# Two weights loaded earlier, residual rows in four pieces and reordered last tiles in an output projection

## The reference, cut to what matters

```python
# end of the first block
merged = jnp.einsum('bsnd,nbsd->bsd', gates, proj)      # three gated branches
out = merged @ w_out[l]                                 # 1024x1024 by 1024x1024
x = x + rms_norm(out, post_norm_w[l])                   # norm over the features
# start of the second block
n = rms_norm_2(h, attn_norm_w[l])
proj = n @ w_in[l]                                      # 1024x1024 by 1024x2816
aq, ak, av, rq, rk, rv, rg = jnp.split(proj, split_at, axis=-1)
aq = rope(rms_norm_2(aq.reshape(B, S, ATTN_HEADS, HEAD_DIM), q_norm_w[l]), pos)
ak = rope(rms_norm_2(ak.reshape(B, S, ATTN_KV_HEADS, HEAD_DIM), k_norm_w[l]), pos)
```

## Time and profile before

| | us |
|---|---|
| median of three executions | 2512.16 |
| the profiled execution | 2513.58 |
| its span, first to last instruction | 2511.6 |
| PE busy, share of the span | 2433.8 (97%) |
| ACT, POOL, DVE busy | 775.0, 847.7, 1072.5 |
| output projection, first matmul to the end of `early(0,1)` | about 1184.8 to 1311.9 |

### The profile page before, as it was taken

The page is one execution under the profiler, slowest core; times in us unless marked ns, Lnnn a source line. Parts: engine busy times, 40 slices in busy tenths (PEclk is TensorE's granted clock), DMA queues, the critical chain, the costliest instruction groups (busy, mean ns, idle before and its releaser), DMA issues. The chain is left out here.

```text
span 2511.6 us, 44136 instructions
## 1 busy us (share of the span) xinstructions
PE 2433.8 (97%) x18612; PEld 1936.5 (77%) x18612; DVE 1072.5 (43%) x1320; ACT 775.0 (31%) x1219; POOL 847.7 (34%) x502
## 2 busy tenths in 40 slices
PE   7999999999999999899989999989999999999999
PEld 6777777777778888687768887767768888887887
DVE  5544222222222334543473537653487666660000
ACT  5332222222221111432351115532453333332210
POOL 1233111111111212243453441064355554555621
PEclk9999999999999999999999999999999999999999
DMA  6336333332131121243432330021513222224431
GB/s 203 125 126 190 87 86 87 86 86 78 49 100 44 57 60 44 91 140 105 153 132 68 92 99 26 14 102 60 168 59 99 85 67 86 94 70 158 146 116 67
DMA packets 258456, 238.82 MB, mean 95 GB/s; under 512 B 35888, under 2 KB 218416, under 8 KB 258160
## 3 DMA queue, kind: packets, MB, share of 16 engines
q1 hardware_dynamic: 251856, 224.80, 28.7%
q10 hardware_dynamic: 6432, 11.54, 1.7%
HBM read 166.80 MB, written 61.90 MB: 91 GB/s over the span
## 5 line engine op out<-in xcount | busy, mean ns | idle before, releaser
L177 POOL TENSOR_TENSOR wlo<-wraw,whi 128x1024 fp32r<-128x1024 f32 x89 | 223.8, 2516 | 701.9 <-ACT whi L172 688.4
L3308 PE MATMUL tl_ps_bank<-tl_dn,tl_hid 128*128 128x512 f32 x792 | 194.4, 390 | 0.0
L172 ACT CAST whi<-wraw 128x1024 fp32r<-128x1024 f32 x89 | 93.2, 1048 | 324.6 <-PE ring L199 127.9
L3308 PEld LDWEIGHTS tl_ps_bank<-tl_dn,tl_hid 128*128 128x128 f32 x792 | 149.1, 188 | 31.1
L2837 POOL TENSOR_TENSOR tl_oplo<-tl_raw,tl_ophi 128x512 fp32r<-128x512 f32 x66 | 106.9, 1621 | 134.4 <-ACT tl_ophi L2832 134.4
L2837 POOL TENSOR_TENSOR tl_oplo<-tl_sum,tl_ophi 128x512 fp32r<-128x512 f32 x88 | 119.5, 1369 | 72.0 <-ACT tl_ophi L2832 72.0
L2845 PE MATMUL tl_ps_bank<-hT_lo,tl_ophi 128*128 128x512 f32 x352 | 113.2, 393 | 2.1 <-POOL tl_oplo L2837 2.1
L2845 PE MATMUL tl_ps_bank<-tl_M,tl_ophi 128*128 128x512 f32 x352 | 112.2, 390 | 0.0
L1023 DVE COPY_PREDICATED rs_X<-rs_level,rs_ps_bank 128x512 f32<-128x512 int32 x40 | 29.6, 739 | 191.4 <-PE rs_ps_bank L1054 191.4
L1075 PE MATMUL lead<-hT_hi,whi 128*128 128x512 f32 x230 | 103.1, 448 | 3.4 <-DVE rs_f_out L989 2.2
L3230 DVE TENSOR_TENSOR tl_res<-lead,tl_res 128x512 f32<-128x512 f32 x4 | 2.8, 692 | 231.5 <-PE lead L3308 231.5
(11 more groups left out here) (499 smaller groups left out, 6219.4 us busy)
## 6 DMA issues: line engine op xcount, KB each, us to landing
wraw<-in_w_in SPq DMA_DIRECT2D x79, 512.0 KB, 4.1
scratch_pg<-rs_f_out SPq DMA_DIRECT2D x48, 256.0 KB, 2.4
wraw<-in_w_out SPq DMA_DIRECT2D x24, 512.0 KB, 4.0
tl_raw<-in_w_gate SPq DMA_DIRECT2D x11, 1024.0 KB, 6.9
tl_raw<-in_w_up SPq DMA_DIRECT2D x11, 1024.0 KB
scratch_hid<-tl_H SPq DMA_DIRECT2D x11, 1024.0 KB, 4.9
tl_hidraw<-scratch_hid SPq DMA_DIRECT2D x22, 512.0 KB, 3.3
tl_dnraw<-in_w_down SPq DMA_DIRECT2D x44, 256.0 KB, 2.8
```

The source lines that it names most:

```text
L172: self.nc.scalar.copy(self.hi[s][:, :], self.raw[s][:, :]).then_inc(self.hi_ready, 1)
L177: self.nc.gpsimd.tensor_tensor(self.lo[s][:, :], self.raw[s][:, :], self.hi[s][:, :].bitcast(F32), ALU.subtract).then_inc(self.lo_ready, 1)
L3308: ins = nc.tensor.matmul(bank[b][:, :], hid[k][:, x, c], dn[n % 2][:, v, :], start=k == 0 and j == 0, stop=k == FF - 1 and j == 2)
```

## The change

It has five parts. (a) `phase_merge` ends with SP loading weight tiles 2 and 3 of the output projection, behind its own last transfers and a wait for its last weight split; `phase_out` begins its loads with tile 4. (b) The residual rows come in four DMAs of 1 MB, one behind each of the weight loads 5 to 8, and POOL waits for all four. (c) ACT evicts tiles 14 and 15 ahead of the casts of weights 16 and 17 (before, only 15), and the chain of slices 4 to 7 stands at t = 14 and 15 instead of 13 and 14. (d) On PE `early(0,0)` waits for each slice of its data instead of for all eight; the sums of the second half stand behind its sixth slice instead of the fourth, the transposes `back(2,1)` behind the second slice of `early(1,0)`; in `early(0,1)` the sum of squares stands ahead of the three matmuls of its slice, and `back(3,0)` ahead of the last slice. (e) In `phase_in2` the waits for the tables move from the start to T = 2 on DVE and behind the second split on POOL.

```diff
--- before.py
+++ after.py
@@ -1550,6 +1550,7 @@
     N, SLOTS = 3 * KD, 4
     with ExitStack() as ctx:
         sh = Shared(nc, ctx, "mg")
+        w.phase(sh)
         b_dram = d.w_branch.rearrange("n (k p) c -> n p k c", p=P)
         piece = lambda t, s: t[:, s * HALF:(s + 1) * HALF]
         raw = [piece(w.raw[s // 2], s % 2) for s in range(SLOTS)]
@@ -1589,6 +1590,9 @@
                         weights(t + SLOTS)
                     if t + 2 < N:
                         gate(t + 2)
+                sp.wait_ge(wl, N)
+                for t in (2, 3):
+                    w.load(sp, t, t % 2, columns(d.w_out, t))
 
             @block.gpsimd
             def _(pool):
@@ -1732,6 +1736,7 @@
         back_ps = [sh.ps(f"back{h}", [P, HALF]) for h in range(2)]
         sum1_ps = [sh.ps(f"sum1{h}", [P, HALF]) for h in range(2)]
         stat = [slice(h * NB, (h + 1) * NB) for h in range(2)]
+        chain = lambda t: {11: (0, 1), 12: (2, 3), 14: (4, 5), 15: (6, 7)}.get(t, ())
         copied, squared, added, summed, root, step, scaled, x1_ready, x_in, stored = (
             sh.sem(n) for n in "copied squared added summed root step scaled x1_ready x_in stored".split())
         widened, returned, squared1, added1, summed1, x1_hi, x1_lo, rms_ready, rms_sum = (
@@ -1740,10 +1745,11 @@
 
             @block.sync
             def _(sp):
-                for t in range(2, N + len(following)):
+                for t in range(4, N + len(following)):
                     w.load(sp, t, t % 2, columns(d.w_out, t % KD) if t < N else following[t - N])
-                    if t == 4:
-                        sp.dma_start(x[:, :, :], d.xT.rearrange("k p s -> p k s")).then_inc(x_in, 16)
+                    if 5 <= t < 9:
+                        k = 2 * (t - 5)
+                        sp.dma_start(x[:, k:k + 2, :], d.xT[k:k + 2].rearrange("k p s -> p k s")).then_inc(x_in, 16)
                 for k in range(KD):
                     sp.wait_ge(x1_ready, KD + k + 1)
                     sp.dma_start(d.x1T[k], x1[:, k, :]).then_inc(stored, 16)
@@ -1754,7 +1760,7 @@
                 def residual(h, k):
                     pool.wait_ge(scaled, h * KD + k + 1)
                     if not k:
-                        pool.wait_ge(x_in, 16)
+                        pool.wait_ge(x_in, 64)
                     nc.gpsimd.tensor_tensor(x1[:, k, half[h]], x1[:, k, half[h]], x[:, k, half[h]], ALU.add).then_inc(x1_ready, 1)
 
                 for t in range(N):
@@ -1792,16 +1798,15 @@
                     nc.scalar.activation(sq1[k % 2] if h or k else total1, x1[:, k, half[h]], ACT.Square).then_inc(squared1, 1)
 
                 for t in range(N):
-                    if t == N - 1:
+                    if t >= N - 2:
                         evict(t)
                     w.split_hi(act, t + 2, t % 2, t // 2 + 1)
-                    if t < N - 1:
+                    if t < N - 2:
                         evict(t)
                     if t == KD:
                         spread_root(0)
-                    if 11 <= t < 15:
-                        for k in (2 * (t - 11), 2 * (t - 11) + 1):
-                            ready(0, k)
+                    for k in chain(t):
+                        ready(0, k)
                 spread_root(1)
                 for k in range(KD):
                     ready(1, k)
@@ -1856,11 +1861,10 @@
                     if 9 <= t < 13:
                         for k in (2 * (t - 9), 2 * (t - 9) + 1):
                             scale(0, k)
-                    if 11 <= t < 15:
-                        for k in (2 * (t - 11), 2 * (t - 11) + 1):
-                            low(0, k)
-                            if t < 14:
-                                accumulate1(k)
+                    for k in chain(t):
+                        low(0, k)
+                        if k < KD - 2:
+                            accumulate1(k)
                 widen(2, small[:, stat[1]], wide[1])
                 for k in (KD - 2, KD - 1):
                     accumulate1(k)
@@ -1892,12 +1896,12 @@
                 def early(T, h, ks):
                     s = w.slot((N + T) % 2)
                     for k in ks:
-                        if h:
-                            pe.wait_ge(x1_lo, KD + k + 1)
-                        ins = half_products(nc, w, ring[2 * T + h], s, hT, k, half[h])
+                        if h or not T:
+                            pe.wait_ge(x1_lo, h * KD + k + 1)
                         if h:
                             pe.wait_ge(squared1, KD + k + 1)
                             mm(sum1_ps[1][:, :], d.ones[:, :], sq1[k % 2], start=k == 0, stop=k == KD - 1).then_inc(summed1, 1)
+                        ins = half_products(nc, w, ring[2 * T + h], s, hT, k, half[h])
                         if k == KD - 1:
                             ins.then_inc(w.product, 1)
 
@@ -1915,20 +1919,20 @@
                         back(1, 0)
                 w.wait_split(pe, N)
                 pe.wait_ge(copied, N - 3)
-                pe.wait_ge(x1_lo, KD)
-                early(0, 0, range(0, 4))
+                early(0, 0, range(0, 6))
                 pe.wait_ge(added, N)
                 sums(1, total[1], summed)
-                early(0, 0, range(4, 6))
-                back(2, 1)
                 early(0, 0, range(6, KD))
                 w.wait_split(pe, N + 1)
                 pe.wait_ge(copied, N)
-                early(1, 0, range(KD))
+                early(1, 0, range(0, 2))
+                back(2, 1)
+                early(1, 0, range(2, KD))
                 pe.wait_ge(added1, KD - 1)
                 sums(0, total1, rms_sum)
-                early(0, 1, range(KD))
+                early(0, 1, range(0, KD - 1))
                 back(3, 0)
+                early(0, 1, range(KD - 1, KD))
         w.end(N)
 
 
@@ -1978,7 +1982,6 @@
 
             @block.gpsimd
             def _(pool):
-                pool.wait_ge(tables, 32)
 
                 def turn(buffer, use):
 
@@ -1987,6 +1990,8 @@
 
                 for T in range(8):
                     w.split_lo(pool, T + 2, T % 2)
+                    if T == 1:
+                        pool.wait_ge(tables, 32)
                     if 2 <= T < 7:
                         turn(*early_place(T - 2))
                     if T == 7:
@@ -2045,7 +2050,6 @@
                 link = Chain(dve, step)
                 dve.sem_inc(copied, 4)
                 link(nc.vector.reciprocal(d.rms[:, half[1]], d.rms[:, half[1]]))
-                dve.wait_ge(tables, 32)
 
                 def empty(T, u, j):
                     for h in range(2):
@@ -2075,6 +2079,8 @@
                         dve.wait_ge(root, T)
                         link(nc.vector.reciprocal(small[:, :], small[:, :]))
                         spread(nc.vector.tensor_copy, wide[:, :], small[:, :]).then_inc(widened, 1)
+                    if T == 2:
+                        dve.wait_ge(tables, 32)
                     if T >= 3:
                         link(nc.vector.tensor_tensor(x_cos[:, :], row(T - 3), cos[:, :], ALU.mult))
                         rotate(T - 3, 0)
```

## The result

The changed kernel took 2493.57 us, median of six executions (2491.51 to 2495.97), and the kernel before 2513.03 us (six executions, the three from ahead of the prediction among them). The ratio is 0.9924, 95% interval 0.9912 to 0.9937: 19 us faster. I had predicted 2495, in 2489 to 2502. The profiled execution took 2493.79 us with a span of 2491.8, that of the kernel before 2513.58 with 2511.6.

The account below looks back on a forecast made before the run. PE bounds the kernel, busy 97%, with 14.6 us of gaps and 10.5 of lower clock. Gains 4.6 + 3.5 + 2.0 + 1.1 + 0.8 + 2.0 + 3.4 = 17.4 us take 2513.58 to 2496.2; median 1.4 lower: 2495, range 2489 to 2502.

Parts of the forecast that it names:

- (a): Ahead of tile 2: early loads of weights 2 and 3 remove a 2.86 us gap and 1.7 of clock, 4.6 us.
- (b): Ahead of tile 5: residual pieces let load 5 land in time, removing 1.83 us gap and 1.7 of clock, 3.5 us.
- Rival 3: Weight loads 6 to 9 land late behind the 1 MB residual pieces, so the kernel becomes slower, 2518; 3%.
- (c), (d), the tail: Last tiles and early(0,0): splits 16 and 17 hold DVE, 2.8 us of gap remains; 3.2 us gained, 2.0 net.
- my signs of being wrong: Late casts 6 to 9, split-caused gap at tile 15 or 16, early(0,1) waits over 0.5 us per slice, gain below 10.
- The transposes: back(2,1) ahead of early(0,1): less PE work covers the chain, a loss between 0 and 2.7 us, taken as 1.2.
- (d), the boundary: Phase boundary: PE's gap falls from 2.20 to about 1.1, gaining 1.1 us, plus 0.8, half of 1.7 us of clock.
- (e): Start of phase_in2: later table waits close the 1.87 us gap before the head sums, 2.0 us, plus 3.4 of clock.
- The sum for the stretch: All gains together, 17.4 us; the stretch runs from the output projection's first matmul to the second head sums.
- Rival 1: Clock stays low at the boundary and behind the head sums, transposes cost 2.7 us: 11.7 us gained, 2500.5; 17%.
- Rival 2: Tail: the two splits don't hold DVE, the chain keeps up and slice 5 is in time: 22.6 us gained, 2489.6; 9%.

Follow-up runs that it names:

- e3: Changed kernel with weights 2 and 3 loaded at the start of the output projection, as before; ratio to the kernel before 0.9938.
- e10: Repeat of e2 with more rounds: changed kernel with the residual rows in one 4 MB transfer; ratio to the kernel before 0.9938.
- e2: Changed kernel with the residual rows in one 4 MB transfer behind weight load 4; ratio to the kernel before 0.9922.
- e4: Changed kernel with ACT's evictions, the chain, and PE's sums and transposes in their old order; ratio to the kernel before 0.9942.
- e7: Changed kernel with only PE's end of the phase as before, each slice's sum behind its products; ratio to the kernel before 0.9945.
- e1: Changed kernel with DVE and POOL again waiting for both tables at the start of phase_in2; ratio to the kernel before 0.9941.
- e5: Changed kernel with only ACT's eviction order and the chain in the tail as before, PE's new order kept; ratio to the kernel before 0.9935.
- e9: Changed kernel with one POOL wait added: split 17 begins only when DVE has written low 7; ratio to the kernel before 0.9918.
- e12: Repeat of e9: changed kernel with split 17 held until low 7 is written; ratio to the kernel before 0.9926.
- e6: Changed kernel with one POOL wait added: split 17 begins only when DVE has the total of tile 15; ratio to the kernel before 0.9935.
- e8: Changed kernel run again without any edit; ratio to the kernel before 0.9930.
- e11: Changed kernel run a third time without any edit; ratio to the kernel before 0.9931.

## Why the prediction was right, step by step

- **(a), 4.6 us**: right. Gap and drop are gone, and e3 brings both back (2.86 + 1.8; 4.8 at the end of tile 15).
- **(b), 3.5 us**: right in its place and size by the trace of after: with (a) it gave 8.55 where I had 8.1, and no cast waited for a DMA. Rival 3 had asked what a weight does behind a piece: 1 MB lands in 6.9 us, and casts 5.44 us apart never waited. Undone alone it costs 2.3 us in the trace of e10 and 6.1 in that of e2 at the end of tile 15, so the 3.5 lie between two outcomes of the clock, and the times don't show it (0.5 +- 2.3).
- **(c), (d), the tail, 2.0 us net**: right in size by the traces (e4 less e7: 4.8 - 2.8 = 2.0; by the start of the next phase 2.3), not told by the times, and right in the cause: both splits hold DVE. Split 17 held the addition ahead of the total from 1272.7, so 2.39 us stood ahead of the sums and 0.18 ahead of slice 5, where I had put 2.3 ahead of slice 5 and 0.5 ahead of the sums. I had let `low` 5 be the held one; it started at 1272.05, 0.3 us ahead of split 17, and got through. Which operation is held differs between traces with the same tail: in e1, e2 and e3 it was `low` 6. The transposes cost 0.64 us of PE (the gap at 1295.58), not 1.2. This, and the 0.24 us that PE waited for split 16 at 1268.98, are small cases of two of my signs of being wrong (over 0.5 us on a slice of `early(0,1)`, a gap at tile 16 for its split); neither changed the sum by more than half a microsecond. And (c) on its own gave nothing (e5): I priced it together with PE's order and could not see that.
- **(d), the boundary, 1.1 + 0.8 us**: 2.20 became 1.02. The clock term was mis-sized: I took half of the 1.7 us, and the trace gave all of it; e4, which has the old gap, has the drop right behind it again.
- **(e), 2.0 + 3.4 us**: right; first head sums 5.77 us behind the phase's start, where I had 5.8 to 7.2, and the clock at 1.00 behind them. With the wait back, e1 has the gap and a drop of 3.4 us again. That the clock stayed up behind the head sums was not certain, though: in e9 and e12 it fell there by 1.6 us without a gap.
- The sum for the stretch was 17.4 and is 18.6; the missing 1.2 us are mainly the other half of the boundary's clock and 0.5 us in (a) and (b). The last 1.2 us between the spans lie outside the stretch and are no larger than the scatter there.
- Rival 1 (the clock stays low) was wrong for this kernel, but it was the right worry: in e7, e9 and e12 the clock did fall right behind the head sums, the stretch of very short matmuls that the rival named. Rival 2 needed the splits not to hold DVE; they did.

## What to carry to other kernels

Price a wait on PE at its length plus what the granted clock loses behind it: here some 9 of 19 us came from the second, and a gap of under 2 us can cost twice its length and more (1.83 + 1.7 and 1.87 + 3.4 us before). Before making a late operation earlier, look at what the waiting engine will wait for next; twice here (e5, e6) a wait taken away at one place stood again at the next, and only holding back the competing operation past the whole chain moved the end. When parts are worth 2 to 4 us and executions scatter by 6, compare marks inside the traces as well as the times, take the mark that lies right behind the part in question, ahead of the next wait, and take two traces where the clock is part of the answer.

## What the runs showed of the hardware

- **The gap's length alone doesn't decide whether the clock falls, or when.** Every gap of 2.20 us or more had a drop in it or behind it, but in e7 it came only 8.5 us behind PE's restart at the boundary, where before and e4 had it within 0.4. Between 1.0 and 2.0 us it went either way: 1.83 us before tile 5 gave 0.83, while 1.96 us there in e10 left 1.00; 0.24 + 1.70 us in the tail left 1.00 in e2 and e3, while the same waits in e1 and 0.24 + 1.57 in e6 were followed by drops of 1.7 us. 1.02 us at the boundary was followed by no drop at all in eight traces; in e9 and e12, with the same gap, PE then worked 8.4 and 8.7 us at 1.00 before the clock fell. The losses come as about 1.7 us or as twice that, for the same gap (e8 and e11). And 1.68 us ahead of the phase's first tile cost nothing in any trace here. I had expected a threshold.
- **A drop with no gap just ahead of it.** In e7, e9 and e12 the clock fell 0.7 to 1.0 us behind the end of the first head sums, sixteen matmuls of two columns in 1.95 us, and PE had been idle for no more than 0.04 us since the boundary. The same sixteen were followed by no drop in the eight traces just named. So it may be these matmuls, the gap further back, or both; no run here tells them apart, and what else decides is open.
- **A VectorE operation beside POOL's split waits for its end.** In the rows of the tail above, a 128x512 addition took 0.68 us free and 2.85 beside a split of 2.66, and ended 0.5 us behind it. In e9 a mere copy of an 8-column operand, 0.43 us free, was held for 2.37 us beside the split of 2.36. This is what the Trainium skill, "SBUF — State Buffer", section "SBUF: two separate sides", says of the port pair that the two engines share, for a VectorE operation with two operands in SBUF or in a two-port mode: "whichever [...] starts first gets the pair for the whole instruction; the other fully blocks". The rows agree, and holding the split back until VectorE is done is what e6 and e9 do. But which of the two is first can't be read from the starts: POOL can lose as well, and in e1, e2 and e3 split 17 took 3.85 us while the addition and the total behind it ran in 0.69 each, though the split's row starts 0.31 us behind that of `low` 5 just as in the changed kernel, and ahead of the addition's. The row of the copy in e9, then those of e2, DVE and POOL:

```profile
1273.32 2.37 DVE L1840 COPY y<-ot_small 128x512 f32<-128x512 f32 x1
```

```profile
1277.62 0.69 DVE L1854 TENSOR_TENSOR rms<-rms,y 128x512 f32<-128x512 f32 x1
1278.22 0.69 DVE L1832 TENSOR_TENSOR y<-y 128x512 f32<-128x512 f32 x1
```

```profile
1277.26 3.85 POOL L177 TENSOR_TENSOR wlo<-wraw,whi 128x1024 fp32r<-128x1024 f32 x1 [3.44 <-ACT whi L172]
```

- **The same 4 MB transfer** landed in 14.2 us (before), 15.0 (e2) and 13.9 (e10). Between e2 and e10 that 1.1 us is the difference of the gaps, 3.03 and 1.96; the clock fell at the first and not at the second, and it fell behind the 1.83 us of before.
